# One encoder layer on one core: the sample's tiles first in attention, out-projection and routing

## The chip, the cores and the metric

The kernel runs on one core of a Trainium2 chip. The metric is the device time of one execution in microseconds (us). TensorE (PE) multiplies matrices, VectorE (DVE) and ScalarE (ACT) work on vectors, GpSimd (POOL) does small vector work and issues the indirect DMAs, SyncE (SP) issues most of the other DMAs. The engines run side by side, each through a list of its own in fixed order, and meet at semaphores.

## The reference

One layer of a hybrid encoder with the same weights for two groups of tokens: a prompt of 256 and a sample of 512, each of width 1024. In float32:

```python
h = rms_norm(x)
p = h @ w_in                                   # one projection for all heads
a = gated_linear_attention(p)                  # 4 heads, forward and backward
d = differential_softmax_attention(p)          # 4 heads, two maps each
x = x + concat(a, d) @ w_out
h2 = rms_norm(x)
aff = softmax(h2 @ w_router)                   # 16 experts
gates, idx = top_k(aff.T, cap)                 # each expert picks its own tokens: 32 of 256, 64 of 512
y[idx] += gates * ((silu(xe @ w_gate) * (xe @ w_up)) @ w_down)     # xe = h2[idx]
```

Attention and the choice of tokens stay within a group. An expert's rows of both groups (96) go through its weights together.

## The kernel before

The 768 tokens lie in six tiles of 128: tiles 0 and 1 are the prompt, 2 to 5 the sample. Precision: each float32 operand is split in a high and a low part, and `three` makes three products of a pair.

**Projection** (L616 to L618 with `HTh`). Units of 128x512; the last slice's units for two tiles are left for attention. In this stage `roped_at` places the turns of rotary results among the units.

**Attention** (loop over `ATT`, 24 rounds of group, tile, head, and four more to drain). Round i on TensorE: the scores of i (L838), a fill from `FILL` (L788, L616 to L618, L808), the turns of the mixed weights of i-3 (L858), and the product with the values of i-4 (L872). On VectorE: the row maxima of i (L1710), the reciprocals of i-1 (L1718), the mixed weights of i-2 (L1726), then `beside(i)`. On ScalarE: the exponentials of i (L1253), the scaling of i-1 (L1263), the copy of the turned weights of i-3 (L1270), of the output of i-4 with its squares (L1279, L1281), then its own side work. A sample round has 512 keys, a prompt round 256.

**Fills.** `FILL` says which work of the projection and the out-projection stands in which round: a unit, a turn of a tile of the linear part (turn), half a tile of its out-projection (half), a turn of the differential part (dturn) or half a tile of its out-projection (dhalf). They take banks 6 and 7 in turn, and `fill` waits until the fill two before it in the list has been read (`fill_read`). VectorE reads halves and turns of the linear part in its own round's `beside`, those of the differential part one round later (L1667, L1674). The loop is:

```python
for x in FILL.get(i, ()):
    if x[0] == "turn":
        gla_turned_low(x[1])
    elif x[0] == "half":
        gla_half_added(x)
for x in FILL.get(i - 1, ()):
    if x[0] == "dturn":
        diff_low(x[1])
    elif x[0] == "dhalf":
        diff_half_added(x[1], x[2])
```

**Out-projection and routing.** After the loop come the differential halves of tiles 2 to 5, between them for each tile the turns of its residual rows (`rows_turned`, L883) and the 16-column router products (`router_logits`, L894). ScalarE and VectorE copy the turned rows (L1307, L1750), take the roots (L1300, L1034) and norm the rows (L1741), which are stored to `h2_dram`. When all six tiles have logits, VectorE takes the softmax of all (L1779 to L1786) and, after two transposes (L919), finds eight times the next eight values and positions for 96 rows at once: 16 experts times two halves of the sample and one of the prompt (L1792 to L1796). Lists of values and indices are transposed (L929, L931), the halves merged (L1807 to L1819), and GpSimd gathers the first expert's rows (`gather`, L558). Meanwhile TensorE runs 64 filler products (`keep_busy`, L924), which compute nothing.

**Experts.** 384 tiles of 1 MB of weights, in eight buffers; ScalarE makes the high part (L1334), VectorE the low one (L1825), TensorE three products each (L949 to L951), the gathered rows are turned at L942. VectorE's first low part waits for `s_issued`, which GpSimd raises after the first gather.

## Time and profile before

| what | value |
|---|---|
| median of 3 runs | 1536.26 us (1536.17 to 1536.48) |
| profiled execution, its own time | 1536.5 us |
| its span in the trace | 1534.7 us |
| mean granted clock of TensorE | 0.995 |

The trace is of one execution. Times in it are counted from the start of the span; about 1.8 us of the execution's own time lie around it. A row of a timeline gives the start, the length and the work, and in brackets how long the engine was idle before it and what released it. The length of a matmul reaches to its modelled end, and the next begins before that, so the spacing of starts is what a matmul costs.

### The profile page before, as it was taken

To read this page: it belongs to the slowest core of one execution; us is meant where nothing else is said; L and a number is where in the kernel's file an instruction comes from. 1 tells how busy PE (TensorE), PEld (TensorE's weight loads), DVE (VectorE), ACT (ScalarE), POOL (GpSimd) and SP (SyncE) were. 2 spreads that over 40 slices of the span, in tenths; PEclk is the share of its full clock that TensorE was granted. 3 is DMA by queue.
4 is the path that set the end of the run, shared out by engine and by line. 5 is a ranking of instruction groups with operands and counts; after the bars stand their busy time and mean duration, and the time that the engine had idled before them with its cause. 6 is when DMAs were issued, how large, how long until landed. Compare 5 with 4: busy or idle time off the path is not lost.

```text
span 1534.7 us, 18598 instructions
## 1 busy us (share of the span) xinstructions
PE 1503.3 (98%) x7293; PEld 1229.7 (80%) x7293; DVE 1245.8 (81%) x1133; ACT 1090.9 (71%) x1230; POOL 140.4 (9%) x105
## 2 busy tenths in 40 slices
PE   7999999999999999999999999999999999999997
PEld 6787777678878888888888888888888888888886
DVE  5348689775588898888989888888988888898985
ACT  7555456875357878787787878778777878778784
POOL 1023131000000101010110101011010101101010
PEclk9999999999999999999999999999999999999999
DMA  6111101402759999999999999999999999999992
GB/s 233 56 55 56 53 3 56 153 28 70 265 197 390 381 387 373 396 378 393 373 384 387 379 395 381 393 372 389 386 376 394 378 393 377 389 384 384 393 373 75
DMA packets 191942, 447.98 MB, mean 292 GB/s; under 512 B 12968, under 2 KB 13296, under 8 KB 191856
## 3 DMA queue, kind: packets, MB, share of 16 engines
q1 hardware_dynamic: 187440, 433.03, 75.7%
q0 software_dynamic: 3968, 12.65, 3.5%
q8 instruction: 58, 0.95, 0.3%
q10 hardware_dynamic: 448, 1.12, 0.2%
q14 instruction: 28, 0.23, 0.0%
HBM read 434.19 MB, written 12.58 MB: 291 GB/s over the span
## 4 chain that ended last, share of the span: by engine, by line
PE 92%; DVE 4%; ACT 2%; issue 1%; DMA 1%; POOLq 0%; POOL 0%; SPq 0%; DVEq 0%; ACTq 0%
PE ps L949 23%; PE ps L951 23%; PE ps L950 23%; PE ps L616 5%; PE ps L618 5%; PE ps L617 5%; PE ps L984 1%; PE ps L838 1%; PE ps L872 1%; DVE states L1491 1%; PE ps L894 1%; PE ps L942 1%; DMA slice_raw<-in_w_in 1%; PE ps L858 1%; ACT wih L1042 1%
## 5 line engine op out<-in xcount | busy, mean ns | idle before, releaser
L1825 DVE TENSOR_TENSOR wl<-raw,wh 128x2048 fp32r<-128x2048 f32 x384 | 873.0, 2289 | 125.9 <-ACT wh L1334 124.5
L1334 ACT CAST wh<-raw 128x2048 fp32r<-128x2048 f32 x384 | 731.2, 1913 | 125.5 <-PE ps L951 123.4
L949 PE MATMUL ps<-wh,XTh 128*128 128x512 f32 x1024 | 404.9, 395 | 0.9 <-issue 0.9
L951 PE MATMUL ps<-wl,XTh 128*128 128x512 f32 x1024 | 399.5, 390 | 0.0
L950 PE MATMUL ps<-wh,XTl 128*128 128x512 f32 x1024 | 398.5, 389 | 0.0
L951 PEld LDWEIGHTS ps<-wl,XTh 128*128 128x128 f32 x1024 | 192.2, 188 | 41.1
L949 PEld LDWEIGHTS ps<-wh,XTh 128*128 128x128 f32 x1024 | 192.3, 188 | 39.0 <-issue 1.1
L950 PEld LDWEIGHTS ps<-wh,XTl 128*128 128x128 f32 x1024 | 192.5, 188 | 38.0
L949 PE MATMUL ps<-wh,gTh 128*128 128x512 f32 x512 | 200.8, 392 | 0.0
L951 PE MATMUL ps<-wl,gTh 128*128 128x512 f32 x512 | 199.4, 390 | 0.0
L950 PE MATMUL ps<-wh,gTl 128*128 128x512 f32 x512 | 199.2, 389 | 0.0
L951 PEld LDWEIGHTS ps<-wl,gTh 128*128 128x128 f32 x512 | 96.1, 188 | 20.3
L950 PEld LDWEIGHTS ps<-wh,gTl 128*128 128x128 f32 x512 | 96.2, 188 | 19.6
L949 PEld LDWEIGHTS ps<-wh,gTh 128*128 128x128 f32 x512 | 96.1, 188 | 19.4
L568 POOL DMA_INDIRECT y_sample<-Ys,tabf x16 | 22.9, 1429 | 923.3 <-ACT Yp L1349 815.5
L616 PE MATMUL ps<-wih,HTh 128*128 128x512 f32 x240 | 95.9, 399 | 1.6 <-DVE slice_low L1399 1.6
L618 PE MATMUL ps<-slice_low,HTh 128*128 128x512 f32 x240 | 93.7, 391 | 0.0
L617 PE MATMUL ps<-wih,HTl 128*128 128x512 f32 x240 | 93.6, 390 | 0.0
L1399 DVE SCALAR_TENSOR_TENSOR slice_low<-slice_raw,st,wih 128x512 fp32r<-128x512 f32 x48 | 33.8, 776 | 45.1 <-ACT wih L1042 45.1
L1354 ACT CAST gTh<-ps 128x384 fp32r<-128x384 f32 x64 | 30.8, 481 | 53.1 <-PE ps L984 52.7
L1375 ACT ACTIVATE hid<-ps 96x512 f32<-96x512 f32 x64 | 38.2, 597 | 35.2 <-PE ps L951 35.2
L616 PEld LDWEIGHTS ps<-wih,HTh 128*128 128x128 f32 x240 | 45.0, 188 | 14.5 <-issue 2.6
(244 smaller groups left out, 1576.3 us busy)
## 6 DMA issues: line engine op xcount, KB each, us to landing
raw<-in_w_gate SPq DMA_DIRECT2D x128, 1024.0 KB, 9.4
raw<-in_w_up SPq DMA_DIRECT2D x128, 1024.0 KB, 9.6
raw<-in_w_down SPq DMA_DIRECT2D x128, 1024.0 KB, 9.7
slice_raw<-in_w_in SPq DMA_DIRECT2D x6, 2048.0 KB, 7.8
X<-in_x_sample SPq DMA_DIRECT2D x8, 512.0 KB, 12.0
slice_raw<-in_w_out SPq DMA_DIRECT2D x2, 2048.0 KB, 8.7
X<-in_x_prompt SPq DMA_DIRECT2D x4, 512.0 KB, 4.2
h_rows<-hn SPq DMA_DIRECT2D x4, 512.0 KB, 3.3
```

The lines of the kernel that those rows point to most:

```text
L568: pool.indirect_dma_start(out=y_sample[0], out_offset=bass.IndirectOffsetOnAxis(ap=sidx[0:CAP_S, e:e + 1], axis=0), in_=Ys[e % 2][0:CAP_S, ...
L616: pe.matmul(out, lh, rh, start=(k == first), stop=False)
L617: pe.matmul(out, ll, rh, start=False, stop=False)
L618: return pe.matmul(out, lh, rl, start=False, stop=(k == last))
L949: pe.matmul(out, hi, rhs_h, start=first, stop=False)
L950: pe.matmul(out, lo, rhs_h, start=False, stop=False)
L951: return pe.matmul(out, hi, rhs_l, start=False, stop=last)
L1334: act.copy(wh[:, n % CONV, :], raw[:, n % RAW, :]).then_inc(s_wh, 1)
L1354: act.copy(gTh[act_buffer(q)][:, :, 0:CAP], ps[:, 6, 0:FC * CAP].rearrange("p (f c) -> p f c", f=FC)).then_inc(s_gth, 1)
L1375: act.activation(hid[0:CAP], ps[0:CAP, TILES[n - 1][1] % 2, :], ACT.Silu).then_inc(s_silu, 1)
L1399: dve.scalar_tensor_tensor(slice_low[n % 2][:, k, :], slice_raw[n % 2][:, k, :], gcol1[:, k:k + 1], wih[:, k, :].bitcast(F32), ALU.mult, A ...
L1825: dve.tensor_tensor(wl[:, n % CONV, :], raw[:, n % RAW, :], wh[:, n % CONV, :].bitcast(F32), ALU.subtract).then_inc(s_wl, 1)
```

## The change

The order of tiles becomes 2, 3, 4, 5, 0, 1 in the last slice's units, in attention, in the out-projection and in routing. `FILL` is laid out anew: the first half of the differential part of the sample's tiles moves into the rounds, with some rounds that hold two fills and some that hold none. The out-projection of the prompt's two tiles is all done after the loop, beside the sample's routing, with the linear and differential part of a half in one bank. The sample's softmax and its eight rounds of top-k stand in VectorE's list among the prompt's low parts and additions; the prompt's softmax and its four rounds follow. Value lists are copied by GpSimd instead of ScalarE, the prompt's indices and gates are turned by VectorE. The normed rows go to two tensors, each expert's gather becomes two indirect DMAs, and the first one of the sample is issued ahead. There are 46 filler products, after the second transposes. Not shown: renamed counts (`POS[t] + 1` for `t + 1`), places of small tables, and lists that are only shortened. The diff, cut to its core:

```diff
@@ -37,17 +37,19 @@
 SLICES = (C_QK, C_V, C_DQ, C_OG, C_DK, C_DV)
 FIRST = 2
 BODY = 4 * NT
-FILL = {1: ("unit", 4, 0), 3: ("unit", 5, 0),
-        6: ("turn", 0, 0), 7: ("turn", 1, 0), 8: ("half", 0, 0), 9: ("half", 1, 0), 10: ("turn", 2, 0),
-        11: ("turn", 3, 0), 12: ("half", 2, 0), 13: ("half", 3, 0), 14: ("half", 0, 1), 15: ("half", 1, 1),
-        16: ("turn", 4, 0), 17: ("half", 2, 1), 18: ("half", 4, 0), 19: ("turn", 5, 0), 20: ("half", 3, 1),
-        21: ("half", 4, 1), 22: ("half", 5, 0), 23: ("half", 5, 1)}
-FILL = {i: [x] for i, x in FILL.items()}
-FILL[21].append(("dturn", 0, 0))
-FILL[23].append(("dturn", 1, 0))
-FILL.update({24: [("dhalf", 0, 0)], 25: [("dhalf", 0, 1)], 26: [("dhalf", 1, 0)], 27: [("dhalf", 1, 1)]})
+ORDER = (2, 3, 4, 5, 0, 1)
+POS = {t: p for p, t in enumerate(ORDER)}
+FILL = {1: [("unit", 0, 0)], 3: [("unit", 1, 0)],
+        5: [("turn", 2, 0)], 6: [("turn", 3, 0)], 7: [("half", 2, 0)], 8: [("half", 3, 0)], 9: [("turn", 4, 0)],
+        10: [("turn", 5, 0)], 11: [("half", 4, 0)], 12: [("half", 2, 1)], 13: [("half", 3, 1), ("dturn", 2, 0)],
+        14: [("half", 5, 0)], 15: [("half", 4, 1)], 16: [("half", 5, 1)], 17: [("dturn", 3, 0), ("dhalf", 2, 0)],
+        18: [("dhalf", 2, 1)], 19: [("dturn", 4, 0), ("dhalf", 3, 0)], 20: [("dhalf", 3, 1)], 21: [("dhalf", 4, 0)],
+        22: [("dhalf", 4, 1)], 23: [("turn", 0, 0), ("dturn", 5, 0)], 24: [("turn", 1, 0)], 25: [("dhalf", 5, 0)],
+        26: [("dhalf", 5, 1)]}
 STEP = {x: i for i, xs in FILL.items() for x in xs}
-HALF_LOWS = {9: (0,), 10: (1,), 11: (2,), 12: (3,), 16: (4,), 17: (5,), 18: (6,), 20: (7,)}
+HALF_LOWS = {8: (0,), 9: (1,), 10: (2,), 11: (3,), 12: (4,), 13: (5,), 14: (6,), 15: (7,)}
+LAST_HALVES = ((0, 0), (0, 1), (1, 0), (1, 1))
+LAST_BANK = {(0, 0): 4, (0, 1): 5, (1, 0): 6, (1, 1): 1}
 EPS = 1e-6
 TAU = 16.0
...
+def tile_at(i):
+    return ORDER[i % NT] if i >= BODY - NT else i % NT
...
 def roped_at(i):
     h, t = i // NT, i % NT
     v0 = h // 2 * NT
     if h % 2 == 0:
-        return {3: (v0,), 4: (v0 + 1, v0 + 2)}.get(t, ())
+        return {3: (v0,), 4: (v0 + 1,), 5: (v0 + 2,)}.get(t, ())
...
                 b = 6 + u - (len(UNITS) - 2)
-            elif kind == "rope" and t % NT < 3:
+            elif kind == "rope" and t % NT < 2:
                 b = 6 + t % 2
             else:
-                b = sum(x[0] != "rope" or x[2] % NT >= 3 for x in UNITS[:u]) % 4
+                b = sum(x[0] != "rope" or x[2] % NT >= 2 for x in UNITS[:u]) % 4
...
-        ATT = [(g, h, t) for g in range(2) for t in range(GROUPS[g][1]) for h in range(HEADS)]
+        ATT = [(g, h, t) for g in (1, 0) for t in range(GROUPS[g][1]) for h in range(HEADS)]
...
+            for t in ORDER[:4]:
+                sp.wait_ge(s_unit, unit_of("tok", len(SLICES) - 1, t) + 1)
+                load_rows(t)
             sp.wait_ge(s_unit, len(UNITS))
-            load_rows(0)
-            load_rows(1)
             load_w_out(1)
-            for t in range(2, NT):
...
+            for t in ORDER[:4]:
+                store_rows(t)
+                store_h2(t)
+            sp.wait_ge(s_mt, NT)
+            load_tile(3)
+            load_tile(4)
+            for t in ORDER[4:]:
+                store_rows(t)
+                store_h2(t)
             for n in range(RAW, NTI):
...
+            def gather_sample(e):
+                pool.indirect_dma_start(out=XE[0:CAP_S, :], out_offset=None, in_=h2_sample,
+                                        in_offset=bass.IndirectOffsetOnAxis(ap=sidx[0:CAP_S, e:e + 1], axis=0))\
+                    .then_inc(s_gat, 16)
+            def gather_prompt(e):
+                pool.indirect_dma_start(out=XE[CAP_S:CAP, :], out_offset=None, in_=h2_prompt,
+                                        in_offset=bass.IndirectOffsetOnAxis(ap=pidx[0:CAP_P, e:e + 1], axis=0))\
...
             def gather(e):
-                if e >= 1:
-                    pool.wait_ge(s_xtp, 2 * e)
-                pool.indirect_dma_start(out=XE[0:CAP, :], out_offset=None, in_=h2_dram,
...
+                gather_sample(e)
+                gather_prompt(e)
...
+            pool.wait_ge(s_clear, 2)
+            pool.wait_ge(s_top, CAP_S // 8)
+            pool.tensor_copy(valr[0:NE, :], topv[0:NE, :])
+            pool.tensor_copy(valr[32:32 + NE, :], topv[32:32 + NE, ::-1]).then_inc(s_vals, 1)
...
+            pool.wait_ge(s_route, 1)
+            pool.wait_ge(s_h2w[0], 16 * 3)
+            pool.wait_ge(s_h2w[1], 16 * 2)
+            gather_sample(0)
+            pool.wait_ge(s_h2w[1], 16 * 3)
             pool.memset(XTh[1][:, :, CAP:P].bitcast(F32), 0.0)
             pool.memset(XTl[1][:, :, CAP:P].bitcast(F32), 0.0).then_inc(s_pad, 1)
-            pool.wait_ge(s_route, 1)
-            gather(0)
+            pool.wait_ge(s_route, 2)
+            gather_prompt(0)
             pool.memset(nlam[:, 1:2], 0.0).then_inc(s_issued, 1)
...
+            pe.wait_ge(s_p, 2 * len(ATT))
+            rows_turned(2)
+            rows_turned(3)
+            pe.wait_ge(s_wtc, len(ATT))
+            gla_half(0, 0, LAST_BANK[0, 0], None)
+            pe.wait_ge(*fill_read(last_in_bank(7)))
+            router_logits(2)
+            rows_turned(4)
+            router_logits(3)
+            rows_turned(5)
+            router_logits(4)
+            pe.wait_ge(s_pvc, len(ATT))
+            gla_half(0, 1, LAST_BANK[0, 1], None)
+            router_logits(5)
+            diff_turned(0)
+            pe.wait_ge(*fill_read(last_in_bank(6)))
+            gla_half(1, 0, LAST_BANK[1, 0], None)
             pe.wait_ge(s_aff, 1)
             for j in range(2):
...
+            mm.then_inc(s_afT, 1)
+            gla_half(1, 1, LAST_BANK[1, 1], None)
+            pe.wait_ge(s_mtd, POS[0] + 1)
+            diff_turned(1)
+            diff_half(0, 0, None)
+            diff_half(0, 1, None)
+            diff_half(1, 0, None)
+            rows_turned(0)
+            router_logits(0)
+            diff_half(1, 1, None)
+            rows_turned(1)
+            pe.wait_ge(s_vals, 1)
+            pe.transpose(ps[0:CAP_S, 7, 2 * P:2 * P + CAP_S], valr, ident[0:CAP_S, 0:CAP_S])
+            pe.wait_ge(s_cand, 1)
+            pe.transpose(ps[0:CAP_S, 7, 2 * P + CAP_S:3 * P], idxr, ident[0:CAP_S, 0:CAP_S]).then_inc(s_topT, 1)
+            router_logits(1)
+            pe.wait_ge(s_aff, 2)
...
-            keep_busy(38)
-            pe.wait_ge(s_vals, 1)
-            pe.transpose(ps[0:CAP, 0, 0:GR], valr, ident[0:GR, 0:GR])
-            pe.wait_ge(s_cand, 1)
-            pe.transpose(ps[0:CAP, 0, GR:2 * GR], idxr, ident[0:GR, 0:GR]).then_inc(s_topT, 1)
-            keep_busy(26)
+            keep_busy(46)
...
-                if i == STEP["dturn", 0, 0] or i == STEP["dturn", 1, 0]:
-                    diff_high(0 if i == STEP["dturn", 0, 0] else 1)
+                for x in FILL.get(i, ()):
+                    if x[0] == "dturn":
+                        diff_high(x[1])
...
+            def rows_inverse_root(v):
+                rows_squared(v)
+                r = st[:, 32 + root_place(v):33 + root_place(v)]
+                ch.link(act.activation(r, st[:, v:v + 1], ACT.Ln, scale=1.0 / D, bias=eps[:, 0:1]))
+                act.activation(r, r, ACT.Exp, scale=-0.5).then_inc(s_rt2, 1)
+            def h2_copied(v, f):
+                p = POS[v]
+                act.wait_ge(s_tr2, 2 * p + f + 1)
+                if p >= 2:
+                    act.wait_ge(s_lg, p - 1)
+                act.copy(h2T[p % 2][:, 4 * f:4 * f + 4, :], ps[:, 2 + f, :].rearrange("p (k c) -> p k c", k=4))\
+                    .then_inc(s_h2d if f else s_h2a, 1)
...
+            act.preload_act_table_set("sqrt_and_others")
+            for v in ORDER[:4]:
+                h2_copied(v, 0)
+                rows_root(v)
...
+            diff_high(0)
+            affinity_exp(afft[:, :, 0:2, 0:NE], 1)
+            diff_high(1)
+            for v in ORDER[4:]:
+                rows_inverse_root(v)
+                h2_copied(v, 0)
+                h2_copied(v, 1)
+            affinity_exp(afft[:, :, 2, 0:NE], 2)
...
+            diff_mixed(0)
+            diff_half_added(5, 0)
+            h2_copied(2)
+            diff_half_added(5, 1)
+            h2_copied(3)
+            rows_normed(2)
+            h2_copied(4)
+            rows_normed(3)
+            h2_copied(5)
+            diff_mixed(1)
+            rows_normed(4)
+            rows_normed(5)
...
+            dve.wait_ge(s_clear, 2)
+            dve.wait_ge(s_lg, 4)
+            affinity_shifted(sample, logit[:, :, 0:2, 0:NE], root_of[:, :, 0:2].unsqueeze(3), stat_of[:, :, 0:2], 1)
+            diff_low(0)
+            affinity_scaled(sample, stat_of[:, :, 0:2], 1)
+            def top_eight(rows, c, values, n, more):
+                dve.max(topv[rows, c:c + 8], values).then_inc(s_top, 1)
+                dve.wait_ge(s_top, n)
+                ch.link(dve.max_index(topi[rows, c:c + 8], topv[rows, c:c + 8], values))
+                if more:
+                    ch.link(dve.match_replace(aff[rows, :], topv[rows, c:c + 8], values, -1.0))
+            both = slice(0, CAP_S)
+            dve.wait_ge(s_afT, 1)
+            for c in range(0, CAP_S, 8):
+                top_eight(both, c, ps[both, 7, 2 * P:4 * P] if c == 0 else aff[both, :], c // 8 + 1, c + 8 < CAP_S)
+                if c == 8:
+                    diff_low(1)
+                elif c == 16:
+                    diff_half_added(0, 0)
+                elif c == 24:
+                    diff_half_added(0, 1)
+                elif c == 32:
+                    root_refined(0)
...
+                elif c == 40:
+                    diff_half_added(1, 0)
+                elif c == 48:
+                    diff_half_added(1, 1)
+            ch.mark(dve.tensor_copy(idxr[0:NE, :], topi[0:NE, :]))
+            dve.tensor_copy(idxr[32:32 + NE, :], topi[32:32 + NE, ::-1]).then_inc(s_cand, 1)
+            root_refined(1)
...
-            dve.tensor_tensor(aff_tok, aff_tok, stat.unsqueeze(2).broadcast_to([P, NT, NE]), ALU.subtract)\
-                .then_inc(s_lmx, 1)
-            dve.wait_ge(s_lex, 1)
-            ch.link(dve.tensor_reduce(stat, aff_tok, AX_X, ALU.add))
...
+            rest = slice(CAP_S, GR)
+            dve.wait_ge(s_afT, 2)
+            for c in range(0, CAP_P, 8):
+                top_eight(rest, c, ps[rest, 2, 0:2 * P] if c == 0 else aff[rest, :], CAP_S // 8 + c // 8 + 1, c + 8 < CAP_P)
+            dve.transpose(pidx[0:CAP_P, :], topi[rest, 0:CAP_P]).then_inc(s_route, 1)
+            dve.transpose(gate[rest, :], topv[rest, 0:CAP_P]).then_inc(s_tables, 1)
```

## Rows read from the trace of the kernel before

**Rows 1.** the page's part 1, busy time of each engine, its share and its instructions
```profile
PE 1503.3 (98%) x7293; PEld 1229.7 (80%) x7293; DVE 1245.8 (81%) x1133; ACT 1090.9 (71%) x1230; POOL 140.4 (9%) x105
```

**Rows 2.** windows: stretch, length, busy us (x instructions) of each engine, clock, DMA share, GB/s
```profile
420.00:440.00 20.00, 16.97 (x63) 13.23 (x64) 16.43 (x60) 6.48 (x7) 2.65 (x10) 0.77 0.18 67
600.00:1500.00 900.00, 900.00 (x4149) 744.56 (x4148) 794.26 (x453) 700.11 (x505) 68.78 (x38) 1.00 1.04 384
```

**Rows 3.** timeline of TensorE, 417 to 443 us: start, length, what [idle before it]
```profile
417.41 2.35 PE L894 MATMUL ps<-wr,h2T 128*128 128x16 f32 x16
421.87 0.66 PE L919 MATMUL ps<-ident,afft 128*96 128x128 f32 x2 [2.12 <-DVE afft L1786]
423.62 11.51 PE L924 MATMUL ps<-wh 128*128 128x512 f32 x38 [1.08 <-ACT wh L1334]
...
435.35 6.16 PE L924 MATMUL ps<-wh 128*128 128x512 f32 x26
441.35 0.82 PE L942 MATMUL ps<-ident,XE 96*128 96x96 f32 x8
443.10 0.47 PE L949 MATMUL ps<-wh,XTh 128*128 128x512 f32 x1 [0.93 <-issue]
```

**Rows 4.** timeline of VectorE: an addition, a norm, softmax and top-k
```profile
414.99 0.69 DVE L1674 TENSOR_TENSOR X<-X,ps 128x512 f32<-128x512 f32 x1 [2.05 <-PE ps L618]
...
418.40 1.29 DVE L1741 SCALAR_TENSOR_TENSOR hn<-X,st,gnorm 128x1024 f32<-128x1024 f32 x1
419.86 0.26 DVE L1779 TENSOR_TENSOR afft<-ps,st 128x96 f32<-128x96 f32 x1 [0.18 <-PE ps L894]
...
421.56 0.26 DVE L1786 TENSOR_TENSOR afft<-afft,st 128x96 f32<-128x96 f32 x1
...
424.53 0.42 DVE L1792 MAX8 tabf<-aff 96x8 f32<-96x256 f32 x1
...
426.03 0.42 DVE L1792 MAX8 tabf<-aff 96x8 f32<-96x256 f32 x1
```

**Rows 5.** timeline of VectorE in round 6 of attention
```profile
282.98 0.69 DVE L1710 TENSOR_REDUCE st<-ps 128x2 f32<-128x512 f32 x1
...
284.24 0.68 DVE L1647 TENSOR_TENSOR MTl<-ps,MTh 128x512 fp32r<-128x512 f32 x1
```

**Rows 6.** timeline of TensorE in attention, turns of weights that waited
```profile
285.89 0.41 PE L858 MATMUL ps<-ident,wmix 128*128 128x128 f32 x2 [0.15 <-ACT wT L1270]
...
301.62 0.63 PE L858 MATMUL ps<-ident,wmix 128*128 128x128 f32 x4 [1.29 <-ACT wT L1270]
```

**Rows 7.** timeline of TensorE in the out-projection
```profile
398.39 1.85 PE L894 MATMUL ps<-wr,h2T 128*128 128x16 f32 x16
400.09 0.49 PE L616 MATMUL ps<-woh,MTh 128*128 128x512 f32 x1
...
402.96 1.04 PE L883 MATMUL ps<-ident,X 128*128 128x128 f32 x8
```

**Rows 8.** timeline of ScalarE at the end of attention
```profile
380.59 0.27 ACT L1279 COPY OD<-ps 128x128 f32<-128x128 f32 x1 [3.09 <-PE ps L872]
...
380.92 0.20 ACT L1281 ACTIVATION_READ_ACCUMULATOR squareD<-ps 128x1 f32 x1
...
381.49 0.21 ACT L1231 ACTIVATE st<-st 128x4 f32<-128x4 f32 x1
...
382.67 1.28 ACT L1314 ACT_TABLE_LOAD   x1
```

**Rows 9.** the gathered rows' tile XE, 395 to 470 us
```profile
L558 POOL DMA_INDIRECT XE<-h_rows,tabf x3: 954/993/1269, 437.1 to 467.0; - x3
...
DMA to landing us min/median/max: 4.0/4.5/7.5
```

**Rows 10.** windows of 1 us around the changes of the clock
```profile
418.00:419.00 1.00, 1.00 (x10) 0.92 (x9) 0.96 (x3) 0.69 (x1) 0.00 (x0) 0.95 0.00 0
...
429.00:430.00 1.00, 1.00 (x6) 0.83 (x5) 0.93 (x4) 0.00 (x0) 0.00 (x0) 0.93 0.00 0
```

348 lines of the change are left out of this document (138 added, 210 removed).

## The prediction

> **What bounds the kernel now.** I read the page first: TensorE is busy for 98% of the span [rows 1]. The windows say where the rest is. Over the 900 us of expert products TensorE is busy for all 900, with the clock at 1.00, while between 420 and 440 us it has 17 of 20 us, at 0.77 [rows 2]. A moment saved before the experts start is a moment off the total, and one lost there is added; afterwards only TensorE counts. The hardware queues move 384 GB/s in that stage, but TensorE waits for none of it there.
>
> The tensor timeline shows what stands before the experts [rows 3]. The last router logits (417.41 + 2.35) end at 419.76, and the first expert product begins at 443.10. These 23.3 us hold 64 filler products, which compute nothing, two pairs of small transposes and eight transposes of gathered rows. VectorE sets their length [rows 4]: the softmax takes 1.96 us (419.86 to 421.82), and eight top-k rounds follow at 1.50 us each (424.53 to 426.03), the last without its replacement. This is what the change takes apart.
>
> The other place is attention, in rounds. A round's first act on TensorE is the scores, and VectorE's list for that round begins with the reduction of these scores; side work (low parts, additions) comes at its end. In one round of the prompt group the reduction starts at 282.98 and the low part ends at 284.92: 1.94 us [rows 5]. Before the change TensorE waits for turned weights in the first rounds, five times for 0.15 to 1.29 us by the idle marks (the shortest and the longest stand in [rows 6]); with the short drains between a copy and the next product I count 5.3 us over the whole of attention, in nine waits.
>
> **The change, part by part.** I lay each engine's list of the new order side by side with durations of this trace, from the first scores on. The tensor work is the same in sum: a half of the projection is 2.87 us (400.09 to 402.96), the row turns of a tile 0.8 (402.96 to the next half), a tile's logits 1.7 (398.39 to 400.09) [rows 7]. So I need only the waits.
>
> *Start of attention.* The large sample rounds now stand first, beside the two projection fills. The waits there (0.5, 0.7, 0.9 and 1.5 us, all for ScalarE's copy of turned weights) come to 3.5 us where all of attention had 5.3. **-1.8 us.**
>
> *Rounds 17 to 23.* Fills alternate between banks 6 and 7, and each waits until the fill two before it has been read. Before, no two fills of which one waits on the same round's VectorE list met: the paired turns stood with halves that are added in their own round. Now turn 3 and the first half of tile 2 both stand in round 17, and VectorE reads them in its list of round 18, behind the reduction of scores 18. The second half of tile 2 in round 18 waits for exactly that. From the end of the scores the wait is the 1.94 us of [rows 5] and 0.15 us until TensorE moves again [rows 6]: 2.2 us with the drain of the scores. Round 19 repeats it with one turn (0.44 us) in between, 1.8; round 20 again, 2.2; round 23 has turn 5 behind the last half of tile 4, and VectorE does the low part of turn 0 first, 2.3. **+8.5 us.** The bounds of this term: 0 if VectorE's side work were already done, 4 x 2.3 = 9.2 if nothing lies beside it. I take the upper part, for each of the four is a fixed order of two lists.
>
> *Rounds 24 to 27.* Before, these held a half each of the differential part. Now rounds 24 and 27 have none, and the chain exponential, mix, turn, copy, product is bare. A product waits for the copy and the squares of the one before, which take from 380.59 to 381.12 [rows 8]. Waits of 0.6, 1.1, 0.5 and 0.9: **+3.1 us.**
>
> *The turned rows of tile 3* wait for ScalarE's copy of tile 2's. That copy now stands behind the last root (to 381.70, 0.6 us behind the squares) and the table load of 1.28 us, where before it was ahead of it [rows 8]. With 0.5 for the last copy of the attention output and 0.6 for the copy itself, less the 0.8 us in which tile 2 is turned: **+2.4 us.**
>
> *The prompt's last two tiles.* ScalarE takes square, logarithm and exponential (1.7 us) ahead of the two copies of turned rows, TensorE waits for copies, residual and value lists by 0.5, 0.6, 0.6 and 0.9: **+2.6 us.** The small transposes that now precede the last logits are 0.4 + 0.5: **+0.9 us.** GpSimd's two copies of 16x64 values are not in the trace; its issue of an indirect DMA takes 0.99 us [rows 9] and the small VectorE operations of routing 0.26 [rows 4]. I take 0.5 us for both, nearer the small operation since they are of its size; at 2 us the last logits would be 1 us later.
>
> *The sample's eight rounds* stand between a low part, four additions (0.69 us each) and a norm (1.29) [rows 4]. They cost TensorE nothing beyond the waits above: 11.5 us of rounds, 5 of side work and some 3 of its waits for TensorE end some 20 us after the first affinities, when TensorE has 20 us of projection to do. The new DVE transposes (32x32) are between nothing and a max of 0.42 us [rows 4]; I take 0.2 each. The first max reads PSUM, and its copy (0.4 us) goes.
>
> *From the last logits to the experts.* Softmax 1.96 and the norm of tile 1 (1.29 us) that stands inside it, less some 0.3 of ScalarE's exponential that it covers: 2.9 [rows 4]. Transposes bring the filler's start to 3.4. The first 38 fillers took 11.5 us, the next 26 went at 0.228 us each [rows 3], so 46 take 13.3: they end at 16.7. The other branch: 2.9, 1.2 for the sample's routes (a copy and five operations of 0.2 us, an estimate from the small ones in [rows 4]), four rounds less a replacement 5.5, two transposes 0.4, issue 0.99 and landing 4.0 us [rows 9] end at 15.0. The filler is later. From the gathered rows' transposes to the first product it is 1.75 us [rows 3]. 18.5 us instead of 23.3: **-4.8 us.** Had the filler full clock throughout, it would end at 13.9 and the gather would decide, 1.7 us earlier.
>
> *At nothing:* the second gather per expert (about 1 us of GpSimd, which is 9% busy [rows 1]; exposed only if it came before the previous rows were turned), the store order on SP (all copies of normed rows are issued 3 us or more ahead of the prompt's gather), loads of tiles 3 and 4 (they land some 10 us before use), the residual's early loads. The rotary turn moved by one unit in the projection stage is 0.44 us of tensor work: between -1 and +1.
>
> Sum: -1.8 + 8.5 + 3.1 + 2.4 + 2.6 + 0.9 - 4.8 = **+10.9 us**. The profiled execution took 1536.5 us (span 1534.7 and 1.8 around it), 0.2 above the median 1536.26. Prediction **1547 us**.
>
> **Rivals.** *The clock falls during the logits.* The mean clock was 0.95 in 418 to 419 us, though TensorE was still issuing logits until 419.76, and 0.93 in 429 to 430 [rows 10]; between them the fillers ran at half speed, 38 in 11.51 us with the fast ones at 0.228 [rows 3]. So it fell from 2.4 to 1.2 GHz some 4 us after the last wide product, among 16-column logits and row turns. In the new order three logits and two turned tiles follow each other with no wide product, 6.7 us. If it falls there, about 10 us at half speed cost some 4 to 5 us: 1551. Against it: the tensor waits of [rows 6], up to 1.29 us, left the clock where it was.
>
> The Trainium skill, "TensorE: Matmul & The Clock Gate", Part 1, says that the throttled state is the default and that activity releases it. By that rule each of the new stops, too, is an invitation to the throttle and the filler has to win the clock back; the trace agrees for the stretch after the last logits.
>
> *The bank waits are mostly hidden.* If VectorE and ScalarE ran ahead so that each cost half, 4.2 us go, and with a filler at full clock 1.7 more: 1541. Nothing in the lists allows the reduction to start before its scores.
>
> *Faster: the routing is what counts.* Place: the end of routing. Four of eight rounds leave it (6.0 us), with copies and list operations (0.4 + 1.0); the filler ends first at full clock. That makes 23.3 to 16.8, -6.5 us, and with the start's -1.8 and the last rounds' +3.5 the time is 1531.7. It decides if the bank waits, the bare rounds and the table load, 14 us in my sum, come to under 1.7 us.
>
> *The change doesn't do what it says:* the sample's top-k is held up by the side work among its rounds (four additions, a low part, a norm, 5 us) until it ends that much later; TensorE would stand before the value transposes: 1552.
>
> **How the numbers follow.** Forecast 0.50 (with its unknowns 1542 to 1550), clock falls 0.22, top-k held up 0.05, waits half hidden 0.13, faster 0.07, and 0.03 for no change at all. The range 1539 to 1552 leaves out the faster case, no change and part of the late ones. A difference of 0.2%, 3.1 us, is what a measurement of this kernel can tell from none. Faster by more 0.07; within 0.07; slower 0.86.
>
> **What the new profile would show.** Right: a tensor wait near 2 us before the differential half or turn of rounds 18, 19, 20 and 23, ended by VectorE's low part or addition; some 2.4 us before tile 3's row turns, behind a table load; the last logits 15 us later than 419.76; some 18.5 us from there to the first expert product; the same speed in the expert stage. Wrong: waits under 1 us in rounds 18 to 23, last logits before 425 us, a clock below 1.00 between attention and the last logits, or an expert stage that differs by over 1 us from 443.1 to the end.

## The result, and the profile after

| what | before | after |
|---|---|---|
| median | 1536.28 us (4 runs, 1536.17 to 1536.48) | 1548.14 us (4 runs: 1547.72, 1548.12, 1548.17, 1551.33) |
| profiled execution, its span | 1536.5, 1534.7 us | 1547.72, 1545.9 us |
| mean granted clock | 0.995 | 0.993 |

The ratio is 1.008, with a 95% interval of 1.0068 to 1.0092: slower by 11.9 us, where 1547 was forecast. Single executions of one kernel after the change differ by several us, so every median below stands with its range. The kernel before ran again beside each group of experiments; its medians were 1536.36, 1536.24, 1536.57 and 1536.05 us, so times of different groups can be laid side by side to about 0.5 us.

TensorE's busy time over the span is what it was (1503.3 us in [rows 1]); GpSimd's rose from 140.4 to 169.2 us, as each expert now has two gathers. The profile's page, part 1, after:

```profile
PE 1503.5 (97%) x7277; PEld 1230.1 (80%) x7277; DVE 1246.9 (81%) x1150; ACT 1091.5 (71%) x1232; POOL 169.2 (11%) x123
```

The windows show where the 11 us are. First the kernel before over attention's second half and the out-projection, then the kernel after (columns as in [rows 2]):

```profile
340.00:360.00 20.00, 20.00 (x108) 14.53 (x107) 13.97 (x30) 14.04 (x42) 0.00 (x0) 1.00 0.04 5
...
380.00:400.00 20.00, 20.00 (x133) 17.94 (x132) 10.89 (x20) 9.18 (x20) 0.00 (x0) 1.00 0.79 286
```

```profile
340.00:360.00 20.00, 16.48 (x99) 12.89 (x97) 7.11 (x19) 9.15 (x35) 0.00 (x0) 1.00 0.00 1
360.00:380.00 20.00, 15.88 (x84) 12.26 (x80) 12.28 (x36) 9.77 (x39) 0.00 (x0) 0.94 0.27 97
380.00:400.00 20.00, 15.63 (x79) 13.08 (x79) 7.56 (x16) 10.97 (x35) 0.00 (x0) 0.89 0.52 188
...
600.00:1500.00 900.00, 900.00 (x4152) 744.73 (x4151) 792.26 (x452) 702.59 (x508) 95.22 (x52) 1.00 1.04 383
```

TensorE, busy for nearly all of these 60 us before (19.46 in the middle 20), now stands for 12 of them, and part of the rest runs at a lower clock. The expert stage is as full as it was. The tensor timeline of the kernel after names each stop:

```profile
348.45 0.50 PE L651 MATMUL ps<-wih,MTh 128*128 128x512 f32 x1 [2.06 <-DVE MTl L1707]
...
355.48 0.50 PE L651 MATMUL ps<-woh,MTh 128*128 128x512 f32 x1 [1.46 <-DVE X L1714]
362.31 0.50 PE L651 MATMUL ps<-wih,MTh 128*128 128x512 f32 x1 [2.06 <-DVE MTl L1707]
...
377.82 1.11 PE L844 MATMUL ps<-ident,OD 128*128 128x128 f32 x4 [2.06 <-DVE X L1714]
...
382.97 0.41 PE L880 MATMUL ps<-ident,wmix 128*128 128x128 f32 x2 [0.99 <-ACT wT L1307]
383.58 0.47 PE L651 MATMUL ps<-woh,MTh 128*128 128x512 f32 x1 [0.20 <-DVE MTl L1707]
391.14 0.68 PE L894 MATMUL ps<-VD,wT 128*128 128x128 f32 x4 [0.72 <-ACT squareD L1315]
395.00 1.94 PE L907 MATMUL ps<-ident,X 128*128 128x128 f32 x8 [2.31 <-ACT h2T L1352]
...
433.40 0.66 PE L907 MATMUL ps<-ident,X 128*128 128x128 f32 x4 [0.40 <-DVE X L1714]
434.56 0.24 PE L954 MATMUL ps<-ident,tabf 64*64 64x64 f32 x1 [0.51 <-POOL tabf L608]
...
435.61 3.59 PE L918 MATMUL ps<-wr,h2T 128*128 128x16 f32 x16 [0.69 <-ACT h2T L1352]
442.09 0.66 PE L961 MATMUL ps<-ident,afft 128*96 128x128 f32 x2 [2.88 <-DVE afft L1815]
442.41 12.36 PE L966 MATMUL ps<-wh 128*128 128x512 f32 x46
454.62 0.82 PE L979 MATMUL ps<-ident,XE 96*128 96x96 f32 x8
456.37 0.47 PE L986 MATMUL ps<-wh,XTh 128*128 128x512 f32 x1 [0.93 <-issue]
```

The four bank waits of rounds 18, 19, 20 and 23 (TensorE waits until VectorE has read the fill that lies in the bank) are the first four rows, 7.6 us in sum; the next three, and one of 0.16 us at 380.37 that is left out, are the rounds with few fills; at 395.00 stands the table load's wait. VectorE's timeline of round 18 shows the order of lists that makes the first wait: the reduction begins at 346.44 and the low part for which TensorE waits ends at 348.40, though VectorE had been idle for 3.69 us before.

```profile
346.44 0.69 DVE L1750 TENSOR_REDUCE st<-ps 128x2 f32<-128x512 f32 x1 [3.69 <-PE ps L864]
...
347.71 0.69 DVE L1707 TENSOR_TENSOR MTl<-ps,MTh 128x512 fp32r<-128x512 f32 x1
```

One row of the first list is out of line with [rows 7]: the last logits (435.61) took 3.59 us where sixteen such products took 1.85. Windows of 1 us of the kernel after show why:

```profile
377.00:378.00 1.00, 0.18 (x1) 0.18 (x2) 0.97 (x4) 0.30 (x2) 0.00 (x0) 0.81 1.05 385
...
394.00:395.00 1.00, 0.00 (x1) 0.03 (x1) 0.01 (x1) 0.99 (x3) 0.00 (x0) 0.84 1.04 406
395.00:396.00 1.00, 1.00 (x5) 1.00 (x6) 0.00 (x0) 0.97 (x3) 0.00 (x0) 0.50 1.06 414
...
435.00:436.00 1.00, 0.39 (x2) 0.39 (x3) 0.48 (x3) 1.00 (x3) 0.00 (x0) 0.82 0.52 201
...
445.00:446.00 1.00, 1.00 (x4) 0.75 (x4) 0.96 (x4) 0.96 (x1) 0.00 (x0) 0.56 0.79 234
```

The clock fell to half (1.2 GHz) three times ahead of the experts: from 377.6 to 381.0, from 394.7 to 398.1, and from 435.6 to 445.9 us. Before, it fell there once, from 418.9 to 429.1 [rows 10]: 0.9 us of it in the last logits, 3.9 in the stops and small transposes up to 423.62, and 5.5 in fillers [rows 3]. The first two new falls begin inside stops of 2.06 and 2.31 us, the third behind the short stops ahead of the last logits. In both profiles the clock falls once more some 4 us behind the last product, where TensorE has nothing left to do.

Laid out by milestones of the two profiled executions: the last logits end at 439.20 (435.61 + 3.59) and not at 419.76, +19.4 us. From there to the first expert product it is 17.2 us and not 23.3, -6.2. First to last expert product takes 1081.2 or 1081.3 us. From the start of the last product to the end of the span it is 8.3 us (1537.64 to 1545.9) and not 10.4 (1524.33 to 1534.7), -2.1. The sum is +11.2, the difference of the spans. From the first scores, which start at 263.74 in both, to the last logits TensorE's idle time rose from 3.3 to 16.5 us and its busy time from 152.7 to 158.9, for the same work and two small transposes: about 13 us of the 19.4 are waits and the other 6 are for the most part products at the lower clock.

### The profile page after: what moved, and what is told of

Its sections match the earlier page's. It is cut to its first block, busy times and chain, and to the rows that moved or that the text cites. A ratio compares the mean times of both kernels' runs of the same rounds, so it can differ in the third digit from the quotient of the medians.

```text
span 1545.9 us, 18649 instructions
## 1 busy us (share of the span) xinstructions
PE 1503.5 (97%) x7277; PEld 1230.1 (80%) x7277; DVE 1246.9 (81%) x1150; ACT 1091.5 (71%) x1232; POOL 169.2 (11%) x123
## 4 chain that ended last, share of the span: by engine, by line
PE 90%; DVE 4%; ACT 3%; issue 1%; DMA 1%; POOLq 0%; POOL 0%; SPq 0%; DVEq 0%; ACTq 0%
PE ps L986 23%; PE ps L988 23%; PE ps L987 23%; PE ps L651 5%; PE ps L653 4%; PE ps L652 4%; PE ps L1021 1%; PE ps L864 1%; PE ps L894 1%; DVE states L1531 1%; PE ps L918 1%; PE ps L966 1%; PE ps L979 1%; ACT wih L1079 1%; DMA slice_raw<-in_w_in 1%
## 5 line engine op out<-in xcount | busy, mean ns | idle before, releaser
L596 POOL DMA_INDIRECT y_sample<-Ys,tabf x16 | 23.3, 1453 | 894.4 <-ACT Yp L1394 845.2
L651 PEld LDWEIGHTS ps<-wih,HTh 128*128 128x128 f32 x240 | 45.1, 188 | 17.2 <-issue 5.2
## 6 DMA issues: line engine op xcount, KB each, us to landing
raw<-in_w_gate SPq DMA_DIRECT2D x128, 1024.0 KB, 11.5
raw<-in_w_up SPq DMA_DIRECT2D x128, 1024.0 KB, 11.5
raw<-in_w_down SPq DMA_DIRECT2D x128, 1024.0 KB, 11.5
```

The costliest lines, as they stand in the source:

```text
L596: pool.indirect_dma_start(out=y_sample[0], out_offset=bass.IndirectOffsetOnAxis(ap=sidx[0:CAP_S, e:e + 1], axis=0), in_=Ys[e % 2][0:CAP_S, ...
L651: pe.matmul(out, lh, rh, start=(k == first), stop=False)
```

## The experiments

My theory after this: the fixed order of lists makes the waits, the waits open the door for the clock, and both together outweigh what the routing saves. Rivals: the waits hide other waits that would take their place; the clock falls for other reasons; the routing saving is nil.

| run | median us | range, runs | ratio to before (95%) |
|---|---|---|---|
| after | 1548.14 | 1547.72 to 1551.33, 4 | 1.008 (1.0068 to 1.0092) |
| e1_read_first | 1542.33 | 1541.84 to 1543.55, 5 | 1.0040 (1.0027 to 1.0053) |
| e2_copy_first | 1548.84 | 1545.04 to 1553.04, 6 | 1.0077 (1.0061 to 1.0093) |
| e3_hold_clock | 1551.56 | 1545.14 to 1551.79, 5 | 1.0089 (1.0075 to 1.0103) |
| e4_filler38 | 1547.82 | 1545.81 to 1550.81, 5 | 1.0081 (1.0068 to 1.0094) |
| e5_copy_early | 1540.44 | 1538.76 to 1543.53, 9 | 1.0029 (1.0019 to 1.0039) |
| e6_logits | 1538.95 | 1537.08 to 1541.06, 11 | 1.0016 (1.0007 to 1.0025) |
| e7_hold_softmax | 1538.17 | 1536.52 to 1539.96, 11 | 1.0015 (1.0006 to 1.0024) |
| e8_topk_last | 1564.18 | 1562.93 to 1567.38, 4 | 1.0188 (1.0172 to 1.0203) |
| e9_act_queue | 1551.12 | 1550.14 to 1554.88, 4 | 1.0093 (1.0077 to 1.0108) |
| e10_rounds | 1537.71 | 1535.51 to 1541.66, 11 | 1.0007 (0.9998 to 1.0016) |
| e11_vector_list | 1535.33 | 1532.86 to 1539.58, 11 | 0.9991 (0.9982 to 1.0000) |
| e12_copies_first | 1533.18 | 1530.96 to 1536.70, 12 | 0.9984 (0.9976 to 0.9993) |

### The bank waits: e1_read_first and e5_copy_early

```diff
+            def read_earlier(i):
+                for x in FILL.get(i - 1, ()):
+                    if x[0] == "dturn":
+                        diff_low(x[1])
+                    elif x[0] == "dhalf":
+                        diff_half_added(x[1], x[2])
+
             for i in range(len(ATT) + 2):
+                read_earlier(i)
                 if i < len(ATT):
                     n = GROUPS[ATT[i][0]][1] * P
```

(The same lines leave `beside`.)

> VectorE takes the low parts and additions of the differential fills (those of round i-1) ahead of the reduction of the scores of round i, not at the end of its list; nothing else is changed. My theory: the four waits of 2.06, 1.46, 2.06 and 2.06 us in rounds 18, 19, 20 and 23 (with drains some 8.3 us) go, since VectorE idles before the reduction of round 18 anyway (3.69 us) and the two reads take 1.4 us while TensorE does turns, a product and the scores. The granted clock no longer falls at 377.7 us, which gives back about 1.5 us more. Time 1538 us (1536.5 to 1540), last logits some 10 us earlier. Rival, the chain of exponential, mix, turn and product is what sets a round: the waits turn up again before the turns of weights, and the time is 1544 or more.

It came to 1542.33 us, 5.8 less and not 10. The tensor timeline tells where the rest is:

```profile
347.98 0.50 PE L651 MATMUL ps<-wih,MTh 128*128 128x512 f32 x1 [1.24 <-DVE MTl L1707]
...
375.06 0.41 PE L880 MATMUL ps<-ident,wmix 128*128 128x128 f32 x2 [1.25 <-ACT wT L1307]
377.77 0.41 PE L880 MATMUL ps<-ident,wmix 128*128 128x128 f32 x2 [1.41 <-ACT wT L1307]
```

In rounds 19 and 23 the wait is gone. In 18 and 20 it is 1.24 and 1.19 us: VectorE now waits for ScalarE's high part, which stands last in ScalarE's round (346.60 to 347.19). The fall of the clock at 377.6 us is gone, as expected; the one at the table load is still there, from 390.3 to 393.7, and begins 0.8 us behind the end of that stop (389.50). And behind the last fills the waits for turned weights grew from 0.16 and 0.99 to 1.25 and 1.41, since these rounds hold nothing else. The next run moves ScalarE's copy:

```diff
...
                     act.mul(wmix[v % 2][:, 0:n], prob[v % 3][:, 1, 0:n], st[:, 164 + b:165 + b]).then_inc(s_cm, 1)
+                for x in FILL.get(i, ()):
+                    if x[0] == "dturn":
+                        diff_high(x[1])
                 if 3 <= i < len(ATT) + 3:
```

(The same lines leave the end of ScalarE's round.)

> As the run with the reads first, and ScalarE also copies the high part of a differential turn ahead of the copy of turned weights in its round, not at the round's end. My theory: the waits of 1.24 and 1.19 us that were left before the halves of rounds 18 and 20 came from this copy, which the low part needs; they go, and with them about 2.4 us: 1540.0 us, where the run before it had 1542.3. The waits of 1.25 and 1.41 us for turned weights after the last scores stay. Rival: the copy of turned weights, now 0.6 us later, makes TensorE wait for it instead; 1542 or more.

1540.44 us, 0.4 above the 1540.0 expected; both waits shrank to 0.33:

```profile
346.96 0.50 PE L651 MATMUL ps<-wih,MTh 128*128 128x512 f32 x1 [0.33 <-DVE MTl L1707]
```

So the two orders of lists cost 7.7 us (1548.14 - 1540.44), and ScalarE's list was part of the wait, not VectorE's alone. The 7.7 us are a balance: 7.0 us of waits gone (7.64 less the 0.33 and 0.33 that are left), a fall of the clock of 3.4 us gone with them, and waits for turned weights behind the last fills that grew. The last are the first rival, which holds for a small part: 1.5 us came back there in the first run (1.25 + 1.41 - 0.16 - 0.99), and about as much in the second (1.74 + 0.99).

### The table load: e2_copy_first

```diff
+            h2_copied(ORDER[0], 0)
             act.preload_act_table_set("sqrt_and_others")
-            for v in ORDER[:4]:
+            rows_root(ORDER[0])
+            for v in ORDER[1:4]:
```

> ScalarE copies the first half of tile 2's turned rows ahead of the table load and not behind it. My theory: the 2.31 us wait before tile 3's row turns shrinks to about 1.0 (the 1.28 us of the load), and if the clock's fall at 394.8 us comes from that stop it goes too, for another 1.5 us: 1545.5 us. Rival, the fall of the clock has nothing to do with the length of this stop: the clock still falls in 394 to 399 us and only 1.3 us are won: 1546.8. Second rival, the wait moves to the root of tile 2 behind the load: no gain, 1548.

```profile
395.39 1.06 PE L907 MATMUL ps<-ident,X 128*128 128x128 f32 x8 [0.88 <-ACT h2T L1352]
...
405.07 3.44 PE L918 MATMUL ps<-wr,h2T 128*128 128x16 f32 x16
```

The wait shrank from 2.31 to 0.88 us, by more than the load's 1.28, and no fall of the clock began in it. Yet this execution was slower, and the median tells no gain; the two fastest executions, at 1545.04 and 1545.07 us, lie where the theory had them (1545.5). Six executions of this one kernel took 1545.04, 1545.07, 1546.43, 1551.24, 1552.98 and 1553.04 us, at mean granted clocks of 0.994, 0.994, 0.992, 0.990, 0.988 and 0.988. Time follows the clock: 0.006 of 1550 us is 18.6 us more at half speed, and they cost 8.0 us, 0.43 us for each. That is an estimate from means rounded to 0.001: the same working gives 0.71 in e3_hold_clock and 0.28 in e8_topk_last, and a single row, the last logits of the kernel after, 0.49 (1.74 us more in 3.56). The profiled one, at 1552.98, had five falls in the part that the change touches, from 348.8, 379.5, 403.4, 434.1 and 440.9 us, and one of 3.4 us at 14.3 us, in the start of the kernel, which cost next to nothing: its first scores start at 263.83 and not 263.74. The fall at 403.4 came among row turns and 16-column logits, with TensorE busy throughout:

```profile
404.00:405.00 1.00, 1.00 (x7) 1.00 (x6) 0.00 (x0) 0.53 (x2) 0.00 (x0) 0.50 0.99 397
```

### The clock by itself: e3_hold_clock and e7_hold_softmax

```diff
+            def hold_clock(n):
+                for _ in range(n):
+                    pe.matmul(ps[:, 4, :], wout_high[1][:, 0, 0:P], wout_high[1][:, 0, 0:512], start=True, stop=True)
+
+            STOPS = {18: 7, 19: 5, 20: 7, 23: 7}
...
+                if i in STOPS:
+                    pe.wait_ge(s_wtc, i - 3)
+                if i in (18, 20):
+                    hold_clock(STOPS[i])
                 if i < len(ATT):
-                    for x in FILL.get(i, ()):
+                    for n_, x in enumerate(FILL.get(i, ())):
+                        if n_ == len(FILL[i]) - 1 and i in (19, 23):
+                            hold_clock(STOPS[i])
                         fill(x)
...
             rows_turned(2)
+            pe.wait_ge(s_wtc, len(ATT))
+            hold_clock(8)
             rows_turned(3)
-            pe.wait_ge(s_wtc, len(ATT))
```

> Filler products of 128x512, which compute nothing, stand in the stops: 7, 5, 7 and 7 of them in rounds 18, 19, 20 and 23 and 8 before tile 3's row turns, at about 0.23 us each, so that each ends about when the wait did. The waits themselves stay. This prices the clock apart from the waits. My theory: the granted clock stays at 1.00 where it fell from 377.7 to 381.1 and from 394.8 to 398.2 us, and the time falls by about 3 us to 1545, while all milestones before 377 stay where they are. Rival, the falls are not caused by the stops: the clock falls at the same places and the time is 1548 or, by what the fillers overrun, up to 1 us more.

```profile
393.88 1.06 PE L919 MATMUL ps<-ident,X 128*128 128x128 f32 x8 [0.46 <-ACT h2T L1365]
```

```profile
394.00:399.00 5.00, 5.00 (x34) 4.49 (x34) 2.05 (x3) 2.90 (x7) 0.00 (x0) 1.00 1.06 391
...
401.00:402.00 1.00, 1.00 (x7) 1.00 (x7) 0.96 (x3) 0.85 (x3) 0.00 (x0) 0.50 1.07 422
```

The two falls at the filled stops are gone (clock 1.00 in 377 to 382 and 394 to 399), and what follows them starts 1.1 us earlier. But from 401.0 to 411.2 the clock was at half in the stretch of logits and row turns, without any stop; in the profile of the kernel after it had stayed at 1.00 there. One of five executions took 1545.14 us, my forecast, the others 1550 to 1552. So the stops are one place where the clock falls and the stretch of logits and row turns another, and the spread of times says that which of them it takes differs between executions of one kernel. The expected gain did not come in the median, and the effect of the stops alone stays open in its size. That the stops cause the falls is not shown either: the two falls went when their stops were filled, but a third came that had no stop.

> As the run with the new order of logits, with nine filler products of 128x512 in the 2.9 us in which TensorE waits for the prompt's softmax. They are off the path of the data. My theory: TensorE's clock falls around the last logits because of the stops there; with fewer stops and this one filled the 10.2 us at half speed that every execution showed between the last logits and the experts is gone or comes later, the 46 fillers take 10.5 us in place of 12.4 and the gather decides: 1.5 us less than the run without them. Rival: the fall begins before this stop (it did at 435.6 us, with the logits themselves), the fillers change nothing or put the small transposes behind them: equal, or up to 1 us more.

This run is built on e6_logits, which comes below. Its nine fillers of 512 columns stand between the last logits and the affinity transposes. 1538.17 us against 1538.95 of the same kernel without them: not to be told from equal. In the profile the clock had fallen at 427.8, inside the last logits, so the fillers ran at half speed:

```profile
426.75 2.69 PE L919 MATMUL ps<-wr,h2T 128*128 128x16 f32 x16 [1.14 <-ACT h2T L1354]
...
429.73 4.21 PE L961 MATMUL ps<-MTh 128*128 128x512 f32 x9
...
434.01 10.98 PE L969 MATMUL ps<-wh 128*128 128x512 f32 x46
```

They outlast the softmax: the transposes behind them start at 433.73, and the 46 that follow give that back (10.98 us where 12.45 were taken without them). The rival, that the fall begins before this stop, fits the profile.

### What the overlap is worth: e8_topk_last, e4_filler38

```diff
             for c in range(0, CAP_S, 8):
-                top_eight(both, c, ps[both, 7, 2 * P:4 * P] if c == 0 else aff[both, :], c // 8 + 1, c + 8 < CAP_S)
...
             rows_normed(1)
             affinity_scaled(prompt, stat_of[:, :, 2], 2)
+            for c in range(0, CAP_S, 8):
+                top_eight(both, c, ps[both, 7, 2 * P:4 * P] if c == 0 else aff[both, :], c // 8 + 1, c + 8 < CAP_S)
...
-            keep_busy(46)
+            keep_busy(60)
+            pe.wait_ge(s_vals, 1)
...
+            keep_busy(34)
```

> The kernel after, with one part undone: the sample's eight rounds of top-k, its lists and their transposes stand behind the prompt's softmax, where they are beside nothing; 94 filler products in place of 46. This prices the overlap that the change was made of. My theory: eight rounds at 1.50 us, the copy and the two transposes come to 12.5 us on the path from the last logits to the experts, and the transposes ahead of the last logits go (-1.4): 1559 us, first expert product about 29.5 us after the last logits in place of 17.2. Rival: the rounds were on the path in the kernel after too, as TensorE waited for the value lists there (0.51 us), so moving them costs less than 8 us: under 1556.

1564.18 us, 16.0 more than after and 5 more than expected. The last logits end where they did (439.3): the transposes ahead of them are gone, but the wait for ScalarE's copy there grew from 0.69 to 1.56 us. The first expert product comes at 470.20, 30.9 us later and not 17.2. But part of that is my own making:

```profile
442.19 15.86 PE L964 MATMUL ps<-wh 128*128 128x512 f32 x60
...
468.41 0.85 PE L982 MATMUL ps<-ident,XE 96*128 96x96 f32 x8 [2.20 <-DMA XE<-h_prompt_rows,tabf]
470.20 0.65 PE L989 MATMUL ps<-wh,XTh 128*128 128x512 f32 x1 [0.93 <-issue]
```

```profile
458.31 0.28 DVE L1882 COPY cand<-ps 64x128 f32<-64x128 f32 x1 [4.76 <-PE ps L971]
```

Sixty fillers were too many, and VectorE stood 4.76 us for the transposes of its lists behind them. Without that the product would come at some 465.4 to 466, 9 us later than in the kernel after. Here TensorE waited 2.20 us for the gathered rows, which landed 3.0 us after GpSimd began the issue (465.36 to 468.41). In the kernel after that issue began earlier against the fillers:

```profile
448.98 0.91 POOL L581 DMA_INDIRECT XE<-h_prompt_rows,tabf  x1 [4.23 <-DVE tabf L1889]
```

With the same 3.0 us its rows landed at about 452.0, 2.6 us before the fillers let TensorE turn them (454.62). Bound by its gather, the kernel after would take 14.6 us (17.2 - 2.6) from the last logits to the experts, and this one without the 4.76 takes 26.1. So the rounds themselves are worth about 11.5 us of the routing's path, an estimate near the 12.5 of my theory. The overlap works. The rival at under 1556 falls.

```diff
-            keep_busy(46)
+            keep_busy(38)
```

> 38 filler products ahead of the experts in place of 46. My theory: the filler, not the gather, sets the start of the experts. The fillers would end 1.8 us earlier, at 452.8 us, when the gathered rows land by my estimate, so the first expert product comes 1.5 to 1.8 us earlier and the time is 1546.5 us. Rival one, the gather decides: no change, 1548.1. Rival two, the fewer fillers leave a stop before the experts in which the clock falls: 1549 or more.

In the profile of this run it is 15.5 us from the last logits (437.46 + 3.49) to the first expert product at 456.41, 1.7 less than after, as expected, and TensorE did not wait for the gather:

```profile
444.15 10.66 PE L966 MATMUL ps<-wh 128*128 128x512 f32 x38
454.65 0.82 PE L979 MATMUL ps<-ident,XE 96*128 96x96 f32 x8
```

So the filler sets the start of the experts. In the median (1547.82, where 1546.5 was expected) nothing of it shows: this profile had falls that the kernel after had not, at 348.9 us and at 14.4 us. With a spread of 5 us, five executions don't resolve 1.7.

### The end of the span: e9_act_queue

```diff
             for t in ORDER[4:]:
                 store_rows(t)
-                store_h2(t)
...
             affinity_exp(afft[:, :, 2, 0:NE], 2)
+            for t in ORDER[4:]:
+                p = POS[t]
+                act.wait_ge(s_hn2, p + 1)
+                act.dma_start(h2_prompt[t * P:(t + 1) * P, :], hn[:, p % 2, :]).then_inc(s_h2w[p % 2], 16)
```

> The kernel after, with the stores of the prompt's two tiles of normed rows issued by ScalarE, as the last two tiles' were before the change, and not by SyncE. This is about the end of the span: from the last product to the end it is 9.9 us before and 7.9 after, in every run, though the last two scatters take the same on GpSimd. Theory: a queue that has been used by ScalarE for large stores makes the end longer; the 2 us come back and the time is 1550 us. Rival: the tensors in memory or the gathers are the cause and the tail stays at 7.9 us: 1548 us.

The last product starts at 1544.72 and the span ends at 1553.1: 8.4 us, as after. The theory falls: issuing these stores from ScalarE's queue does not bring the 2 us back. The 3 us of time come from elsewhere: the fillers waited 1.17 us for ScalarE's first high part, which now stood behind the wait for a norm, and the profile had five falls of the clock from 378.9 us on, and one at 13.7. The rival, that the tensors in memory or the gathers are the cause, was not tested. What the traces add is the place: before the change the queues move nothing any more from 1532 us on, though the span ends at 1534.7, while after it they move 102 GB/s in 1543 to 1545 and the span ends at 1545.9.

```profile
1532.00:1534.00 2.00, 0.00 (x0) 0.00 (x0) 0.00 (x0) 0.00 (x0) 0.00 (x0) 0.50 0.00 0
```

```profile
1543.00:1545.00 2.00, 0.00 (x0) 0.00 (x0) 0.00 (x0) 0.00 (x0) 0.00 (x0) 0.50 0.69 102
```

So the 2 us that went stood behind the last bytes stored. Why stays open.

### The way back under the kernel before: e6, e10, e11, e12

```diff
             rows_turned(2)
-            rows_turned(3)
             pe.wait_ge(s_wtc, len(ATT))
             gla_half(0, 0, LAST_BANK[0, 0], None)
+            rows_turned(3)
...
             rows_turned(5)
-            router_logits(4)
             pe.wait_ge(s_pvc, len(ATT))
             gla_half(0, 1, LAST_BANK[0, 1], None)
+            router_logits(4)
             router_logits(5)
```

(Not shown: the value and index transposes behind the last logits, and ScalarE's copies between the square and the root.)

> On top of the earlier copy, the order after attention is changed: the first half of tile 0 stands between the row turns of tiles 2 and 3, its second half between the row turns of tile 5 and the logits of tile 4, the transposes of the sample's value and index lists stand behind the last logits (in another bank) and not ahead of them, and ScalarE copies the turned rows of tiles 0 and 1 between the square and the root. My theory: the 2.31 us wait behind the table load is filled by a product that had to be done anyway (-2.3), the transposes and the wait of 0.51 leave the path to the last logits (-0.9) and the wait of 0.69 shrinks to 0.2 (-0.5), so 1536.3 us, and with one fall of the clock fewer 1534.5. Rival: the sample's routing becomes the bound, as every product ahead of the last sample logits delays VectorE's rounds; then the wait for the lists grows by what TensorE gains and the time stays at 1539 or more.

1538.95, 1.5 us less and not 4, as the rival had it. The 2.31 us at the table load are filled, but TensorE waited 1.14 us for the sample's softmax and 1.43 for the last addition, and the wait of 0.69 ahead of the last logits, which was to shrink, grew to 1.14. VectorE's timeline had the cause, a norm that waits for a store to leave its buffer, ahead of the softmax in the list:

```profile
400.04 1.28 DVE L1787 SCALAR_TENSOR_TENSOR hn<-X,st,gnorm 128x1024 f32<-128x1024 f32 x1 [2.96 <-DMA h_sample_rows<-hn]
...
402.51 1.29 DVE L1787 SCALAR_TENSOR_TENSOR hn<-X,st,gnorm 128x1024 f32<-128x1024 f32 x1 [1.12 <-DMA h_sample_rows<-hn]
```

The next puts the halves of tile 5 ahead of the turns of weights:

```diff
-                if i < len(ATT):
+                if i < len(ATT) or i > len(ATT):
                     for x in FILL.get(i, ()):
                         fill(x)
```

> As the run with fillers in the softmax's stop, and the differential halves of tile 5 stand ahead of the turns of weights in the two rounds after the last one of fills, not behind them. My theory: the waits of 1.74 and 0.99 us for turned weights, part of my term for the bare rounds, are covered by 2.9 us of products each: 2.7 us earlier at the end of attention, and 1535.4 us in all. Rival: VectorE's list behind the last sample logits is the bound by then, and what attention gains comes back as waits before the last row turns: 1537.5 or more. The chance falls of the clock move single executions by up to 3 us either way.

1537.71 us, 0.5 less, too little to tell from none and not the 2.7 expected: the second wait (0.99) is gone, the first (1.73) stays, since its round holds only a turn, which I had overlooked.

```diff
             diff_mixed(1)
-            rows_normed(4)
-            rows_normed(5)
+            inverse_root(4)
+            inverse_root(5)
...
                 elif c == 32:
-                    root_refined(0)
-                    rows_normed(0)
+                    rows_normed(4)
...
+            rows_normed(5)
+            diff_half_added(1, 1)
+            root_refined(0)
+            rows_normed(0)
             root_refined(1)
```

(Not shown: SyncE's new order of stores.)

> On top of the former, VectorE takes the norms of tiles 4 and 5 behind the sample's softmax (one among the rounds, one after them), and the last addition, the root and norm of tile 0 after the rounds; SyncE stores two of the tiles after the loads of weights 3 and 4. My theory: VectorE began the sample's softmax 2.6 us after the last sample logits since it waited for stores of normed rows to leave their buffers (2.96 and 1.12 us), and later stood 2.70 us for a root; without these the waits of TensorE before the affinity transposes (1.14 us) and the last row turns (1.43 us) go: 2.5 us less than the run before it, 1533 us, below the kernel before the change at 1536.3. Rival: the late norms hold up the lists of values, and TensorE waits for these behind the last logits: equal.

1535.33 us, 2.4 less than the run before it, where 2.5 less were expected; it is not the 1533 that was written down, as the run before had come out higher itself. With the norms behind the softmax, neither of TensorE's two waits was left over 0.4 us. The last version:

```diff
-                rows_squared(v)
                 h2_copied(v, 0)
                 h2_copied(v, 1)
+                rows_squared(v)
                 rows_inverse_root(v)
...
-            keep_busy(46)
+            keep_busy(42)
```

(Not shown: the turn of tile 1 ahead of the turns of weights in its round.)

> On top of the former: ScalarE copies the turned rows of tiles 0 and 1 ahead of the square; the turn of tile 1 stands ahead of the turns of weights in its round; 42 filler products and not 46. My theory: the wait of 1.14 us before the last logits shrinks to about 0.5 (the square's 1.06 leaves it, and VectorE had 1.68 us to spare for the root), the wait of 1.73 for turned weights to 1.3, and with the four fillers 0.9 us go, as the gathered rows land before the fillers end (the prompt's gather was issued at 438.2 and the fillers ended at 442.5): 1533.5 us, where the run before it had 1535.3. Rival: the gather is as late as the fillers, and the shorter stops change nothing since the clock is at half speed around the last logits anyway: 1535 us.

1533.18 us, where 1533.5 was expected. It is faster than the kernel before by 2.9 us (ratio 0.9984, 0.9976 to 0.9993) and than the change as made by 15.0. The wait of 1.73 us in the round with the turn became two of 0.37 and 0.71, and the one ahead of the last logits is gone, but the one ahead of the last row turns grew from 0.34 to 1.21. Its tensor timeline between the last row turns and the experts:

```profile
427.54 0.66 PE L908 MATMUL ps<-ident,X 128*128 128x128 f32 x4 [1.21 <-DVE X L1717]
428.03 1.90 PE L919 MATMUL ps<-wr,h2T 128*128 128x16 f32 x16
...
433.52 0.43 PE L964 MATMUL ps<-ident,afft 128*96 128x128 f32 x2 [1.08 <-DVE afft L1824]
433.85 9.82 PE L969 MATMUL ps<-wh 128*128 128x512 f32 x42
...
445.26 0.47 PE L989 MATMUL ps<-wh,XTh 128*128 128x512 f32 x1 [0.93 <-issue]
```

From the end of the last logits (429.93) it is 15.3 us to the experts, 8.0 less than before the change. This execution took 1536.6 us; seven of the twelve took 1531.0 to 1533.9, five 1536.4 to 1536.7. In it the clock was at half from 390.8 to 397.6 and from 401.1 to 407.9, and between 383 and 408 us TensorE did not stop once. So falls come in this stretch of logits and row turns without a stop in it:

```profile
391.00:392.00 1.00, 1.00 (x6) 1.00 (x7) 0.95 (x1) 0.36 (x2) 0.00 (x0) 0.50 1.09 334
```

## Why the prediction was right

*The waits of rounds 18, 19, 20 and 23.* Forecast 2.2, 1.8, 2.2, 2.3 us, measured 2.06, 1.46, 2.06, 2.06 by the idle marks, which leave the drains out. Undoing them gave 7.7 us where 8.5 were forecast, but as a balance: 7.0 us of waits, a fall of the clock that went with them, and about 1.5 us that came back behind the last fills. The step named only VectorE's list; ScalarE's copy, last in its own, held 1.8 us of it (1.24 + 1.19 less 0.33 twice). The step also took the 0.15 us of [rows 6] for the time until TensorE moves again, where it is an idle mark; here TensorE started 0.05 us after the low part (348.40 and 348.45).

*Start of attention.* Four waits, forecast 0.5, 0.7, 0.9 and 1.5, measured 0.38, 0.44, 0.62 and 1.25 by the marks, 2.7 us in sum. But the term of -1.8 us did not come: the five waits of the kernel before come to 2.7 us by the same marks, and to 3.25 with one of 0.54 at 363.59, so -0.6 at most. The prediction took 5.3 us for the old ones, with drains; up to 340 us the windows show TensorE idle for 2.8 us before and 2.7 after. The rotary turn, put between -1 and +1, was worth nothing: the first scores start at 263.74 in both.

*Rounds 24 to 27.* Forecast 0.6, 1.1, 0.5 and 0.9, marks 0.16, 0.99, 0.20 and 0.72: 1 us less than the term of 3.1.

*Table load.* Forecast 2.4, mark 2.31; the pieces named in the prediction add up to 2.2 (0.6 + 1.28 + 0.5 + 0.6 - 0.8). *Last two tiles.* Forecast 2.6, marks 0.24, 0.40, 0.51 and 0.69, 1.8 in sum.

*Last logits.* Forecast 15.7 us later, measured 19.4. The waits came out some 1.6 us under my terms (idle time up by 13.2 us, where the terms for waits had 14.8), so 5 to 6 us are missing. TensorE's busy time up to there rose by 6.2 us, of which the prediction had 0.9. The half-speed time is 3.4 + 3.4 + 3.6 us; at the 0.43 us for each that the six executions gave, 10.4 us cost 4.5, an estimate. This is the rival "the clock falls during the logits", whose mechanism was right and whose place was not: in the profile the first two falls began in stops, the third with the last logits, and the stretch of three logits and two turned tiles stayed at 1.00. In two other kernels (e2 and e3) it fell in just that stretch, and in e12, which has a half of the projection in it, twice. My argument against it, that waits of up to 1.29 us had left the clock where it was [rows 6], did not reach to stops of 2 us. The Trainium skill, "TensorE: Matmul & The Clock Gate", Part 1, says that the throttled state is the default, and that the point at which the clock rises at the start of matmul work varies from run to run. If that holds for falls in the middle of a kernel too, one kernel may take several times, and the runs agree (1545.04 to 1553.04 us for one kernel).

*From the last logits to the experts.* Forecast 18.5 us, measured 17.2: the fillers took 12.36 us and not 13.3, as they began when the clock had been down for some 7 us already, and the last logits' slow products lie on the other side of the mark. That the filler, not the gather, decides was right; 38 fillers gave 1.7 us.

*The end.* -2.1 us in the tail were not forecast and are not explained.

*Two of my own signs of being wrong came true:* the clock was at half from 394.7 to 398.1 us, between attention and the last logits, and the time from the first expert product to the end of the span differs by 2.1 us (1089.5 where it was 1091.6), all of it in the tail.

So 1547.0 against 1548.14 is the work of the mechanisms named, and in part of luck. By stages the spans differ from the forecast by +3.7 us up to the last logits (19.4 for 15.7), -1.3 from there to the experts and -2.1 in the tail: errors of up to 3.7 us that leave +0.3. Some 4.5 us of clock that the sum did not hold were offset by smaller waits, a shorter filler and the tail. The rival "waits half hidden" is out (marks of 7.6 us where 8.5 were forecast), "top-k held up" is out as well: TensorE stood 0.51 us for the value lists. The rival "faster: the routing is what counts" had its saving nearly right, -6.5 forecast and -6.2 measured, though not by its own path (the fillers decided, and the clock fell ahead of the mark instead of behind it), and its condition was not met: bank waits, bare rounds and table load came to 12 us by the marks, not to under 1.7.

## What to carry to other kernels

When side work of one round is read in the next, count from the reader's list, not from its load: VectorE had idled for 3.69 us before the reduction behind which the low part stood. Moving the read, and ScalarE's copy, ahead of the round's main step gave 7.7 us, although some 1.5 us came back in the next wait of the chain. A change that opens stops of 2 us on an otherwise full TensorE may also open chances for its clock to fall, though it fell without a stop as well; look at the spread of the executions beside the median. Where a stop has to be filled, take products that must be done anyway first: moving halves into the stops (e6_logits, with other moves) came out 1.5 us faster, while products that compute nothing showed no gain in e3_hold_clock and e7_hold_softmax. No run compares the two in the same stop.

## What was not expected of the hardware

The 78 executions of the kernel before in the five groups lie within 1.6 us (1535.8 to 1537.4), while those of the kernels after the change spread over 1.7 us (e1_read_first, five of them) to 8.0 us (e2_copy_first). Only one execution of each kernel has a trace, so that the place of the falls differs between executions is read from their times and mean clocks. TensorE at half speed for 1 us cost 0.43 us by the estimate from e2_copy_first, with 0.28 to 0.71 in others. The clock also fell where TensorE had been busy without a stop, on row turns and 16-column products: in the kernel before at 418.9, in e2 at 403.4, in e3 at 401.0, in e12 at 390.8 and 401.1.
